# Expert gathers of a PEER layer issued in pairs of rows: U, U, V, V in place of U, V, U, V

## The reference, cut to what matters

```python
def _peer(h, wq, keys, u, v):
    """Product-key retrieval over P_EXPERTS single-neuron experts. h (B,T,D)."""
    def blk(xi):                                  # 128 tokens
        q = (xi @ wq).reshape(P_TOKBLOCK, P_HEADS, 2, P_DQ // 2)
        s = jnp.einsum('nhcd,hckd->nhck', q, keys).astype(F32)
        sv, si = lax.top_k(s, P_TOPK)             # 16 of 128, for each of 8 heads and 2 halves
        ...
        fv, fi = lax.top_k(cand, P_TOPK)
        eidx = jnp.take_along_axis(cidx, fi, -1)  # 16 experts of 16384 per token and head
        gw = jax.nn.softmax(fv, -1)
        ue = jnp.take(u, eidx, axis=0)
        ve = jnp.take(v, eidx, axis=0)
        act = jax.nn.gelu(jnp.einsum('nd,nhkd->nhk', xi, ue).astype(F32), approximate=False)
        return jnp.einsum('nhk,nhkd->nd', gw * act, ve.astype(F32))
```

## Time and profile before

| | |
|---|---|
| runs, us | 6319.0, 6320.56, 6321.11; median 6320.56 |
| profiled execution, us | 6324.11 |
| its span, us | 6322.4 |
| first and last gather of U and V, layer 0 and 1, us from the span's start | 1429.27 to 3157.95 and 4588.54 to 6296.41 |

### The profile page before, as it was taken

How to read it: one execution, slowest core, us unless ns; L and a number is a source line. 1 busy time by engine, 2 the same in 40 slices (tenths; PEclk the granted TensorE clock), 3 DMA queues, 4 the chain that set the end, 5 groups by cost and what they waited for, 6 DMA issues and landing times. The chain is left out here.

```text
span 6322.4 us, 68907 instructions
## 1 busy us (share of the span) xinstructions
PE 5155.5 (82%) x24692; PEld 3512.5 (56%) x24692; DVE 3383.0 (54%) x7425; ACT 1396.0 (22%) x3134; POOL 3274.5 (52%) x3108
## 2 busy tenths in 40 slices
PE   6978867985888888788869788689958888888887
PEld 5767867983444444343357678679834444444432
DVE  3365534127666666666433655341276666666663
ACT  2231223111222122122222312231112221122221
POOL 2123410226777777777721234102167777777775
PEclk8888988998999999999978889889989999999999
DMA  4310011229999999999933100112299999999998
GB/s 141 121 43 8 1 41 45 70 93 332 409 403 400 397 391 401 374 391 393 387 127 121 43 8 1 41 48 68 96 340 407 402 399 401 390 404 393 405 404 347
DMA packets 507342, 1530.52 MB, mean 242 GB/s; under 512 B 57442, under 2 KB 155698, under 8 KB 504692
## 3 DMA queue, kind: packets, MB, share of 16 engines
q0 software_dynamic: 369536, 1342.48, 54.4%
q1 hardware_dynamic: 134804, 181.44, 8.6%
q10 hardware_dynamic: 2656, 2.11, 0.1%
HBM read 1520.75 MB, written 5.09 MB: 241 GB/s over the span
## 5 line engine op out<-in xcount | busy, mean ns | idle before, releaser
L2070 PE MATMUL pb<-vb,x_diags 128*128 128x512 f32 x5120 | 2499.8, 612 | 654.6 <-DMA vb<-in_p_v,x_idx 635.2
L1867 DVE CUSTOM_DVE_ANT_0 ub<-ub,h 128x1024 f32<-128x1024 f32 x1280 | 1567.4, 1225 | 1097.3 <-DMA ub<-in_p_u,x_idx 1087.5
L2070 PEld LDWEIGHTS pb<-vb,x_diags 128*128 128x128 f32 x5120 | 874.7, 190 | 1555.2 <-issue 1314.5
L1806 POOL DMA_INDIRECT ub<-in_p_u,x_idx x1280 | 1310.7, 1024 | 485.5 <-issue 362.5
L1806 POOL DMA_INDIRECT vb<-in_p_v,x_idx x1280 | 1298.6, 1015 | 409.4 <-issue 287.0
L2036 PEld LDWEIGHTS pb<-h2T,Wq 128*128 128x128 f32 x2560 | 459.5, 192 | 504.4 <-issue 501.5
L1990 ACT ACTIVATE x_diags<-identity,x_coefs 128x128 f32<-128x128 f32 x1280 | 416.5, 392 | 555.3 <-PE pb L2070 498.9
L2036 PE MATMUL pb<-h2T,Wq 128*128 128x128 f32 x2560 | 471.1, 276 | 2.4 <-DMA Wq<-in_p_wq 1.7
L239 PE MATMUL pb<-e_Whi,hS_hi 128*128 128x256 f32 x1280 | 382.3, 299 | 28.2 <-DVE e_Wlo L1688 28.2
L240 PE MATMUL pb<-e_Wlo,hS_hi 128*128 128x256 f32 x1280 | 359.2, 281 | 0.0
L241 PE MATMUL pb<-e_Whi,hS_lo 128*128 128x256 f32 x1280 | 358.9, 280 | 0.0
(11 more groups left out here) (403 smaller groups left out, 7880.9 us busy)
## 6 DMA issues: line engine op xcount, KB each, us to landing
adaW<-in_ada_w SPq DMA_DIRECT2D x40, 1024.0 KB, 10.3
e_Wg<-in_w_in SPq DMA_DIRECT2D x24, 1024.0 KB, 6.1
ub<-in_p_u,x_idx POOLq DMA_INDIRECT x1280, 6.6
vb<-in_p_v,x_idx POOLq DMA_INDIRECT x1280, 6.5
m_W<-in_w_in SPq DMA_DIRECT2D x16, 1024.0 KB, 5.7
Wq<-in_p_wq SPq DMA_DIRECT2D x8, 2048.0 KB, 17.2
g_W<-in_w_in SPq DMA_DIRECT2D x10, 1024.0 KB, 5.4
yT<-in_ada_w SPq DMA_DIRECT2D x8, 1024.0 KB, 5.5
```

Source lines behind the costliest of these rows:

```text
L1806: G.indirect_dma_start(ring[:, n % RING, :], None, table, bass.IndirectOffsetOnAxis(ap=idx[:, i % LIVE, s:s + 1], axis=0)).then_inc(in_[n ...
L1867: V.tensor_tensor_reduce(out=ub[:, n % RING, :], in0=ub[:, n % RING, :], in1=h2[:, t, :], scale=1.0, scalar=0.0, op0=ALU.mult, op1=ALU.add ...
L2070: last = mm(pb[2 * (t % 2) + j][:, :], diag[:, n % DRING, :], vb[:, n % RING, 512 * j:512 * j + 512], start=(h == 0 and s == 0), stop=(h = ...
```

## The change

The loop that issues the gathers takes two rows in a step. It issues U rows n and n + 1 and then V rows n - 24 and n - 23. The waits within a gather, the rings, the lag, and all other engines are as they were. 640 + 24 is even, so that no row is left out.

```diff
-                        for n in range(PTOP * NG + LAG):
-                            if n < PTOP * NG:
-                                gather(n, table_u, ub, u_in, x_dot)
-                            if n >= LAG:
-                                gather(n - LAG, table_v, vb, v_in, x_vmm)
+                        for n in range(0, PTOP * NG + LAG, 2):
+                            for k in (n, n + 1):
+                                if k < PTOP * NG:
+                                    gather(k, table_u, ub, u_in, x_dot)
+                            for k in (n, n + 1):
+                                if k >= LAG:
+                                    gather(k - LAG, table_v, vb, v_in, x_vmm)
```

## The result

The changed kernel takes 6686.34, 6700.35 and 6712.39 us, median 6700.35, against 6320.56: ratio 1.060, 95% interval 1.0567 to 1.0634. It is 380 us slower; the forecast was 223 us. The profiled execution is the one of 6686.34 us, 362.2 above that of before.

The account below looks back on a forecast made before the run. Bound: POOL's back-to-back gather issue, lengthened by dots. Cadence 1.245 + 0.098 (second dots) + 0.070 (first dots) = 1.413 us against 1.3225, times 2456 gathers +222, with the tail +223: about 6544 us median; range 6318 to 6715.

Parts of the forecast that it names:

- What bounds the stage: Expert stage: POOL issues gathers back to back, no semaphore holding it; next start at max(own start + 1.245, dot's end + 1.11).
- Ring waits, index waits, clock at no cost: Expert stage: slack 6 us for U and 3.5 for V, index waits unmoved, clock already full; cost 0.
- The tail: End of each layer, PE-bound: V row 614 issued one slot later, costing 0.45 us a layer, 1 us in all.
- Second dots: Second dot of each pair lengthens the next gather by distance less 1.245: 3.13 us per 16-row group, bounds 2.61 and 3.66.
- s=12: Pair at row 12 of a group: second dot 2.45 us after the first, after the gather's start; hold 0.
- The pairs without a piece (s=0 and 14): Pairs with no routing piece between their dots: second dot 1.28 us after the first, hold 0.04 us each.
- The s=4 pair: Pair at row 4: distance 2.29, 0.05 from the edge of 2.34; hold 1.05 or 0, so half taken, 0.52 us.
- First dots: First dot's own hold on a gather: 0.28 us on every second dot, 0.07 per gather; bounds 0.023 and 0.124.
- the restless stretch: Part of the old kernel's expert stage with cadence 1.388 us per gather, where dots hold gathers 0.28 us per dot.
- rival (3): Expert stage: holds move every first dot's phase at random, so the bound of +394 us is reached, 6715 us; chance 0.08.
- Rival (1), the queue: A full descriptor queue holds POOL in the expert stage, so issue order does nothing; no change, 6321 us; chance 0.12.
- Rival (2), faster: Paired dots catch fewer gathers if second dots start over 2.34 us after first; -63 us, 6258 us; chance 0.08.

Follow-up runs that it names:

- the sums: Dot replaced by a plain one-operand sum of the gathered row, product with h2 left out: 6257.87 us in the changed kernel, 6249.45 us in the kernel before.
- PSUM: Whole dot kept, h2 copied once per token tile to PSUM and read there: 6264.96 us in the kernel before, 6266.38 us in the changed kernel.
- the two runs with added work: Changed kernel with useless VectorE sums added behind the pieces of rows 6, 8, 10 and 12: 6305.52 us; of rows 6 and 8 alone: 6555.14 us.
- the plain DMA: Changed kernel with each indirect gather replaced by a plain DMA of 128 rows in a row, choice of experts left out: 6264.19 us.

## Why the prediction was right or wrong, point by point

- **What bounds the stage**: right. POOL's issues, lengthened by dots, with no wait on a ring; shown by the sums and by PSUM, which remove the holds and bring both orders to one time. The rule max(own start + 1.245, dot's end + 1.11) held within 0.06 us for 1246 of the 1334 gathers of the changed kernel that start during a dot, as with 1.84 and 1.91 us where it gives 1.83 and 1.90; nearly all of the others started within 0.04 us of the dot.
- **Ring waits, index waits, clock at no cost**: right for the waits, none over 0.3 us. The tail is 44.89 us of products in place of 43.17, 26 rows (104 entries) in a run in place of 25, 1.7 us more and not 0.45; too small to matter.
- **Second dots**: 3.13 us per group forecast, 3.98 measured, above the upper bound of 3.66. Rows 7, 9 and 11 came out nearly as worked out (0.87, 0.79, 0.60 for 0.87, 0.87, 0.60), and row 3 with 0.16 for 0.19. The error is s=12, taken at distance 2.45 and hold 0, measured 2.22 and 0.89: the 2.45 is the start of a dot that stood 0.14 after the end of the piece, which is at 2.31 in the kernel before. 2.31 would have been wrong as well, since it lies at the edge. The last instruction of this piece (L1864 in the changed kernel) is one that the dot doesn't wait for: the dot of 5393.92 starts while that instruction, from 5393.77 for 0.23 us, still runs. By the rule 2.22 would have given 0.98. The pairs without a piece (s=0 and 14) were set at 1.28 and 0.04 and stand at about 1.5 to 1.8 and 0.27, probably since the second row of U is itself issued late when its gather or the one before is held. The s=4 pair, taken half, costs 0.13. In us of the whole, over 2456 gathers: +68, +35 and -30.
- **First dots**: 0.28 us per dot taken from the restless stretch, 0.41 measured: +79 us. This is the largest part of the miss, and it lies toward rival (3), whose even phase gave 0.495. The term was borrowed from a stretch of the old order, and no row there showed what it would be in pairs; the two runs with added work show that it depends on the second dots before it, which the sum took as separate.
- **The sum**: +222 us forecast against +362 between the profiled executions. 140 us were missing, and the four parts named above sum to +152; rows 3 and 9, which came out lower than set, take 8 off, and the rest lies within the reading of the holds. The range held in part by luck: 6700 lies above the 6650 that the prediction names as the upper end of its likeliest case, an end that no sum there gives. Only the bound of +394, with every first dot at even phase, reaches it, and that was left to rival (3) at a chance of 0.08. The direction, the cause and the rule were right; both terms of the sum were set too small.
- **Rival (1), the queue**: wrong in its reason, as the sums show, but it named the real floor: at 1.292 us per gather the DMA engines do decide, not at the 1.2 us of the estimate. The Trainium skill (SBUF — State Buffer, "Who interferes with whom") reports that a tensor_tensor did not stall DMAs in a probe; the plain DMA here agrees, with 0.605 us at most. Its general rule, that a VectorE instruction with two SBUF inputs contends with a GpSimd instruction that reads SBUF, would cover the indirect form if that is what is held, which no run here shows by itself.
- **Rival (2), faster**: its point of decision, a distance of 2.34 us, was right, as the added work shows; the change by itself leaves six of the eight pairs well under it and that of s=4 on it, at 2.33. Once the dots are placed well, U U V V is indeed faster than the kernel before, 6280 us.
- **Details that were wrong**: the long gathers were expected to be V's; in the changed kernel both tables have them, U's more (1.211 against 1.106 us, where 1.11 was expected on average). The DMA share was expected at 0.94 and is 0.97 and 0.96.

## What to carry to other kernels

Where POOL issues indirect gathers back to back beside VectorE, compare the starts of long gathers with VectorE's instructions of two SBUF operands; if their ends follow, one operand in PSUM, or another placing of the work, is worth more than the order of the DMAs. Before the order of transfers is changed, ask which engine's work their landings start, and at what that work will then be aimed. A distance for such a sum is not to be read from the start of an instruction that a landing may have released, and the end of the work in between is right only where the program waits for that work.

## What the runs showed of the hardware that was not expected

- A plain DMA of 512 KB took POOL 0.53 us and was never held; an indirect one of the same size took 0.945 us and was held for up to 1.06 us.
- Which of the two starts first decides, and within a narrow stretch: a gather up to 0.04 us behind the dot's start was not held, and the dot took 1.26 to 1.30 us instead of 1.23; from 0.045 us on the gather was held in full. A dot that started later during a gather cost neither anything.
- Adding 1.9 us of VectorE work per group (0.42, 0.42, 0.69 and 0.35) made a kernel 395 us faster.
- Time to landing is a poor sign of trouble: 11.4 to 12.6 us in the two runs with the plain sum, the fastest, and 6.2 to 6.3 in the changed kernel, the slowest. In the fast ones POOL does wait for its rings, up to 2 us at a time, and it costs nothing, since the DMA engines are the bound.
- The mean granted clock of TensorE in the stage fell from 0.99 and 1.00 to 0.95 and 0.96 in the changed kernel, which puts part of the time at the lower of its two levels (1.2 GHz); TensorE's busy share had fallen from 83% to 75%. With the dots in pairs in the old order it was 76% from 5000 to 6000 us and the clock 0.99, so the share alone doesn't tell. The lower clock cost nothing that shows: POOL never waited over 0.3 us.
